# The compressor's gathered input in a fused two-model kernel: eight additions and a fill per mixer, moved from VectorE to GpSimd

## What is computed

```
def _compress(x, pe, w1, w2):
    S_ = x.shape[2]
    nc = (S_ - CMP_LEN) // CMP_STRIDE + 1
    idx = jnp.arange(nc)[:, None] * CMP_STRIDE + jnp.arange(CMP_LEN)[None, :]
    blocks = x[:, :, idx] + pe
    flat = blocks.reshape(blocks.shape[0], blocks.shape[1], nc, CMP_LEN * HEAD_DIM_2)
    return jax.nn.silu(flat @ w1) @ w2
...
k_cmp = _rope(_compress(kv(kc), pe[0], w1[0], w2[0]), cmp_end)
v_cmp = _compress(kv(vc), pe[1], w1[1], w2[1])
```

## Time and profile before

| | |
|---|---|
| median of 3 runs | 2712.3 us (2712.06 to 2714.15) |
| the profiled execution, its own time | 2713.11 us |
| span of its profile | 2711.8 us |
| PE busy | 2672.0 us, 99% of the span |
| DVE busy | 1630.6 us, 60% |
| ACT busy | 1023.0 us, 38% |
| POOL busy | 14.1 us, 1% |
| mean granted TensorE clock | 0.997 of full speed |

### The profile page before, as it was taken

How to read it: one execution, slowest core, us unless ns; L and a number is a source line. 1 busy time by engine, 2 the same in 40 slices (tenths; PEclk the granted TensorE clock), 3 DMA queues, 4 the chain that set the end, 5 groups by cost and what they waited for, 6 DMA issues and landing times.

```text
span 2711.8 us, 35115 instructions
## 1 busy us (share of the span) xinstructions
PE 2672.0 (99%) x14437; PEld 2197.6 (81%) x14437; DVE 1630.6 (60%) x3267; ACT 1023.0 (38%) x1757; POOL 14.1 (1%) x43
## 2 busy tenths in 40 slices
PE   8999999999999999999999999999999999999999
PEld 5788888889888888666888889888889666888888
DVE  7766555356767556687776746763346777633334
ACT  4642332435222234565422224322234565422223
POOL 1000000000000000000000000000000000000000
PEclk9999999999999999999999999999999999999999
DMA  8255433133655334411555524543224421233331
GB/s 253 91 173 168 113 95 117 63 109 109 216 187 187 109 103 121 128 32 32 186 186 186 186 90 144 187 142 106 94 90 121 126 63 32 69 103 93 99 99 67
DMA packets 345352, 330.56 MB, mean 122 GB/s; under 512 B 13410, under 2 KB 334694, under 8 KB 345192
## 3 DMA queue, kind: packets, MB, share of 16 engines
q1 hardware_dynamic: 344820, 327.77, 38.8%
q10 hardware_dynamic: 372, 0.55, 0.1%
HBM read 319.89 MB, written 2.10 MB: 119 GB/s over the span
## 4 chain that ended last, share of the span: by engine, by line
PE 93%; DVE 5%; ACT 1%; DMA 0%; SPq 0%; issue 0%; DVEq 0%
PE bank L537 26%; PE bank L539 26%; PE bank L538 26%; PE bank L591 3%; PE bank L2408 1%; PE bank L2437 1%; PE bank L565 1%; PE bank L566 1%; PE bank L567 1%; DVE w_lo L505 1%; PE bank L1395 1%; PE bank L2049 1%; PE bank L1385 1%; DMA mw<-in_w_mod 0%; DVE E L2532 0%; PE bank L874 0%
## 5 line engine op out<-in xcount | busy, mean ns | idle before, releaser
L537 PE MATMUL bank<-h_lo,w_hi 128*128 128x512 f32 (+1 forms) x2432 | 917.4, 377 | 3.6 <-DVE h_lo L716 2.2
L539 PE MATMUL bank<-h_hi,w_lo 128*128 128x512 f32 (+1 forms) x2432 | 894.4, 368 | 0.0
L538 PE MATMUL bank<-h_hi,w_hi 128*128 128x512 f32 (+1 forms) x2432 | 892.6, 367 | 0.0
L505 DVE TENSOR_TENSOR w_lo<-raw,w_hi 128x1024 fp32r<-128x1024 f32 (+1 forms) x420 | 488.9, 1200 | 324.6 <-ACT w_hi L499 324.5
L499 ACT ACTIVATE w_hi<-raw 128x1024 fp32r<-128x1024 f32 (+1 forms) x420 | 419.7, 1035 | 345.9 <-PE bank L539 327.9
L537 PEld LDWEIGHTS bank<-h_lo,w_hi 128*128 128x128 f32 x2432 | 458.3, 188 | 87.0 <-issue 8.2
L538 PEld LDWEIGHTS bank<-h_hi,w_hi 128*128 128x128 f32 x2432 | 458.8, 189 | 76.2 <-issue 4.8
L539 PEld LDWEIGHTS bank<-h_hi,w_lo 128*128 128x128 f32 x2432 | 457.7, 188 | 77.1
L537 PE MATMUL bank<-a_lo,w_hi 128*128 128x512 f32 (+1 forms) x1056 | 391.0, 370 | 0.0
L539 PE MATMUL bank<-a_hi,w_lo 128*128 128x512 f32 (+1 forms) x1056 | 384.7, 364 | 0.0
L538 PE MATMUL bank<-a_hi,w_hi 128*128 128x512 f32 (+1 forms) x1056 | 384.1, 364 | 0.0
(11 more groups left out here) (319 smaller groups left out, 2560.8 us busy)
## 6 DMA issues: line engine op xcount, KB each, us to landing
swf<-in_w_ada SPq DMA_DIRECT2D x60, 1024.0 KB, 8.0
raw<-in_ffn_w_gate SPq DMA_DIRECT2D x44, 1024.0 KB, 5.4
raw<-in_ffn_w_up SPq DMA_DIRECT2D x44, 1024.0 KB, 5.4
raw<-in_w_in SPq DMA_DIRECT2D x40, 1024.0 KB, 5.1
raw<-in_ffn_w_down SPq DMA_DIRECT2D x32, 1024.0 KB, 5.1
raw<-in_w_in SPq DMA_DIRECT2D x32, 512.0 KB, 5.1
raw<-in_ffn_w_down SPq DMA_DIRECT2D x16, 768.0 KB, 4.6
mw<-in_w_mod SPq DMA_DIRECT2D x8, 1024.0 KB, 11.8
```

What stands on the lines that cost most here:

```text
L505: nc.vector.tensor_tensor(o, r, half(w_his[place_of[i]], i, h)[0].bitcast(F32), ALU.subtract).then_inc(*w_lo.up((i, h)))
L537: nc.tensor.matmul(o, w1, al, start=start, stop=False)
L538: nc.tensor.matmul(o, w1, ah, start=False, stop=False)
L539: return nc.tensor.matmul(o, w2, ah, start=False, stop=stop)
```

## The change

`dve_gx` becomes `pool_gx`: the same fill and the same eight additions per mixer, with the same operands and the same waits, issued by GpSimd. Both calls stand in `pool_mixer` between the fill of `kcz` and the multiplications by the triangle. They disappear from `dve_mixer`, where `steps(3)` is left of the spread call. TensorE's wait in `pe_hidden` is now on GpSimd's counter.

```
-    def dve_gx(l, m):
+    def pool_gx(l, m):
         for mm in range(2):
-            dve.wait_ge(act, ("xa", l, mm))
+            pool.wait_ge(act, ("xa", l, mm))
         if m == 0:
-            dve.wait_ge(pe, ("t", ("f", l, 0), 7, 1))
+            pool.wait_ge(pe, ("t", ("f", l, 0), 7, 1))
         else:
-            dve.wait_ge(pe, ("hb", l, 0))
+            pool.wait_ge(pe, ("hb", l, 0))
         gxr = gx[:, :].rearrange("p (r g c) -> p r g c", r=16, g=2)
         if m == 0:
-            nc.vector.memset(gxr[:, :, :, 31:32], 0.0).then_inc(*dve.up(("gx0", l)))
+            nc.gpsimd.memset(gxr[:, :, :, 31:32], 0.0).then_inc(*pool.up(("gx0", l)))
         for g in range(2):
             xv = xa[:, m * 512 + g * 256:m * 512 + g * 256 + 256].rearrange("p (c r) -> p r c", r=8)
             for q in range(2):
                 pv = V(f"pe{l}{m}", 8 * q, 8).unsqueeze(2).to_broadcast((128, 8, 31))
-                nc.vector.tensor_tensor(gxr[:, 8 * q:8 * q + 8, g, 0:31], xv[:, :, q:q + 31], pv, ALU.add).then_inc(
-                    *dve.up(("gx", l, m) if (g, q) == (1, 1) else ("gx", l, m, g, q)))
-                yield
+                nc.gpsimd.tensor_tensor(gxr[:, 8 * q:8 * q + 8, g, 0:31], xv[:, :, q:q + 31], pv, ALU.add).then_inc(
+                    *pool.up(("gx", l, m) if (g, q) == (1, 1) else ("gx", l, m, g, q)))
...
-        pe.wait_ge(dve, ("gx", l, m))
+        pe.wait_ge(pool, ("gx", l, m))
...
-        for _ in dve_gx(l, 0):
-            pass
         dve_gates(l)
...
         dve_rope(l, 7)
         dve_hidden(l, 0)
-        gx1 = dve_gx(l, 1)
-        for i in range(3):
-            steps(1)
-            next(gx1)
-        for _ in gx1:
-            pass
+        steps(3)
         dve_hidden_silu(l, 0)
...
         nc.gpsimd.memset(kcz[:, :], 0.0).then_inc(*pool.up(("zn", l)))
+        pool_gx(l, 0)
+        pool_gx(l, 1)
         pool.wait_ge(ld_ws, l)
```

## The result

The changed kernel takes 2719.24 us (median of 11 runs, 2718.01 to 2720.83) against 2713.38 us for the kernel before beside it (11 runs, 2711.83 to 2715.13): a ratio of 1.0023, 95% interval 1.0015 to 1.0031. It is slower by 5.9 us, 4 to 8 us by the interval. Predicted were 2718.0 us and + 5.7 us. The profiled execution took 2720.21 us, with a span of 2718.9 us.

The account below looks back on a forecast made before the run. TensorE was taken as the bound, busy 2672.0 of 2711.8 us. Both calls' removals and the first call's addition counted 0; the second's cost + 5.7 us over two mixers, 2712.3 + 5.7 = 2718.0 us, range 2716.6 to 2721.7 us.

Parts of the forecast that it names:

- The first call at 0: Call m = 0, before the first scores: moving it costs and gains 0, covered by some 4.8 us of VectorE idle time.
- The gain of the removed additions at 0: Second call, steps 10 to 12: VectorE would wait 1.8 us for ScalarE instead of 0.61 us; the 3.44 us wait stays.
- The block holds both ways: Second call: two-input VectorE instructions and GpSimd instructions reading SBUF block each other, whoever comes second; without it the sum is 0.
- The sum of 2.85 us per mixer: Second call: one GpSimd addition before each of L2029, L2032 and L505, 3 x 0.95 us, all reaching TensorE.
- how long one addition takes on GpSimd: One strided addition of the second call: 0.71 us lower bound, 1.17 us upper bound, middle taken, 0.95 us.
- a second fall of the clock: If a wait passes 3.4 us, clock falls again in each mixer: 9.4 + 6.8 = 16 us, 2728 us, outside the range.
- Rival 1: Second call: VectorE keeps the port and GpSimd stays shut out until L2124; + 1 us, 2713.3 us, chance 0.20.
- rival 2: Second call: no contention that VectorE notices, both halves of the edit off the path; 2712.3 us, chance 0.14.
- rival 3: Additions at 1115.31: freed time shortens the 3.44 us wait to 2.3 us, clock stays up; 9 us faster, 2703.3 us, chance 0.06.

Follow-up runs that it names:

- e1: Kernel before with only the first call (m = 0, with the fill) on GpSimd, the second left on VectorE: 2713.38 us against 2712.92 us, ratio 1.0002.
- e2: Changed kernel with the first call back on VectorE, only the second (m = 1) on GpSimd: 2716.52 us against 2712.92 us for the kernel before, ratio 1.0012.
- e3: Changed kernel with GpSimd's second call held until VectorE has read step 10's scores: 2713.19 us against 2712.92 us for the kernel before, ratio 1.0003.
- e6: Changed kernel with the second call's four additions made twice: 2719.28 us against 2712.94 us for the kernel before, ratio 1.0023.
- e8: e3 and e7 together: 2713.30 us against 2712.94 us for the kernel before, ratio 0.9999.
- e10: e3 with both low parts (L505) ahead of step 13, then steps 13 and 14, then the rotations: 2712.03 us against 2713.37 us, ratio 0.9998.
- e7: Kernel before with VectorE's step 14 ahead of the rotation and low part L505, nothing on GpSimd: 2711.34 us against 2712.94 us, ratio 0.9996.

## Why the prediction was right, point by point

**The first call at 0: right** at the place that it spoke of. e1 shows both halves: VectorE is held up, and the 2.55 us of idle time behind it are left untouched. Some 0.36 us appear further on, in the first mixer alone.

**The gain of the removed additions at 0: right.** The 3.44 us wait stayed at 3.44 us in the changed kernel, in e1, in e2 and in e3. VectorE's wait for ScalarE at the start of this chain grew from 0.61 us to 0.91 us in the changed kernel, less than the 1.8 us I had named, because VectorE now reached step 13's second score early enough to wait for TensorE's transposes there (0.45 us on L591):

```profile
1122.94 0.56 DVE L2124 CUSTOM_DVE_ANT_0 E<-bank,res 128x384 f32<-128x384 f32 x1 [0.45 <-PE bank L591]
...
1124.42 0.62 DVE L2137 SCALAR_TENSOR_TENSOR E<-E,small,E 128x384 f32<-128x384 f32 x1 [0.91 <-ACT E L2154]
```

**The block holds both ways: right**, the step that only a rule stood behind. Rows 7 and 8 had shown one direction; L2026 at 1.24 us is the other.

**The sum of 2.85 us per mixer: right in its total to some tenths, wrong in its parts.** I had 3 turns of 0.95 us. There were 4 turns of 0.53 us on average in the changed kernel, 2.1 us. The step that was off is "how long one addition takes on GpSimd": the stride costs GpSimd nothing (0.73 us undisturbed, my lower bound was 0.71 us), and VectorE waits only for the element part, which I had not thought of taking apart. The count of 3 was a matter of hundredths of a microsecond; e2 has 3, the change has 4. That 2.85 us came out so near is therefore partly luck: a price too high by 0.4 us was made up for by one turn more and by what follows. Two terms that I had not put in fill the sum to the measured lag of 2.49 and 2.86 us:
- 0.36 us in the first mixer. VectorE starts L2137 of step 4 that much later, while ScalarE's times there are the same. It is so in all six profiles that have the first call on GpSimd (the changed kernel, e1, e3, e6, e8, e10) and in none of the seven others, and in the first mixer alone. Before and in e1:

```profile
1076.44 0.35 DVE L2137 SCALAR_TENSOR_TENSOR E<-E,small,E 128x128 f32<-128x128 f32 x1 [0.45 <-ACT E L2154]
```

```profile
1077.69 0.35 DVE L2137 SCALAR_TENSOR_TENSOR E<-E,small,E 128x128 f32<-128x128 f32 x1 [0.80 <-ACT E L2166]
```

  Before, it starts 0.10 us after the scaling (L2154) that it waits for, and in e1 only when ScalarE's next exponential (L2166) has ended too, though the program doesn't ask for that. Why stays open.
- the clock in the second mixer, below.

**The clock.** I had put a second fall of the clock at the upper end only, since a wait of 2.89 us had left it up. In the changed kernel's second mixer it fell after the two short waits of step 10. The busy times and clock of that stretch (columns as in rows 10):

```profile
2140.00:2144.00 4.00, 3.88 (x12) 3.09 (x13) 3.28 (x10) 1.73 (x5) 0.00 (x0) 0.57 0.95 258
```

and in the first mixer, after the same waits, it did not:

```profile
1108.00:1112.00 4.00, 3.73 (x21) 2.62 (x21) 3.50 (x13) 1.74 (x7) 0.00 (x0) 1.00 0.62 161
```

So neither the length of one wait nor the sum of these two says whether the clock falls; it fell after waits of 1.11 and 0.40 us in one mixer and stayed in the other. What decides is not shown here. It costs 0.43 of 4 us of TensorE's time at most, 1.7 us, of which VectorE's lateness at step 11 hides a part: no wait is left there in the second mixer. The second mixer lags by 2.86 us; 2.1 us of that are the turns, and the 0.36 us are absent there, so about 0.7 us are left for the clock.

**The range and the rivals.** Rival 1 (VectorE keeps the port) and rival 2 (no contention that VectorE notices) fell with the timeline of the changed kernel, rival 3 with the unchanged 3.44 us. I had rested rival 3's price on the clock staying up once the wait is under 2.9 us. That was wrong as a price: in e7, whose two waits are 0.38 and 2.77 us, the clock fell in both mixers, and it gained 1.6 us with an interval that takes in zero, and not the 9 us of that sum.

## What to carry to other kernels

Work that is moved off a busy engine to an idle one starts when its own inputs are ready, not where it had stood; look at what the chain of waits does at that new moment. Where VectorE is on the chain with instructions that read two SBUF tiles, each GpSimd instruction that reads SBUF beside it holds up one of them by its element time (at most 2.3 ns an element here), and one wait that let GpSimd begin a few microseconds later took that cost away here. A TensorE wait that VectorE's order causes often reappears a few instructions on when the order alone is changed: 3.44 us became 2.77 and then 2.67 us at the next reader.

## What the runs showed of the hardware that was not expected

- A strided read (31 elements at steps of 32 bytes) takes VectorE 0.63 us for 248 elements, but GpSimd 0.73 us, on the same slope as its dense 128x128 of 0.46 us. For this operation GpSimd is only 16% slower.
- A VectorE instruction on 128x1 elements, usually 0.16 us, took 0.57 us in e6 behind one GpSimd read. The hold goes by GpSimd's length, not by VectorE's.
- The clock fell in one mixer and stayed in the other after the same two short waits (1.11 and 0.40 us in the changed kernel, about 1.1 and 0.81 us in e6).
